# One transformer block pair on one core: the mixer's work put in another order, with the SSD beside the input projections and attention beside memory panels and half of w_out

## The chip, the core and the metric

The kernel runs on one core of a Trainium2 chip. The metric is the device time of one execution in microseconds (us), here the median of three executions. PE is the matrix engine, ACT the scalar engine, DVE the vector engine, POOL the general-purpose engine, SP the queue that issues the loads.

## What is computed

Two blocks on 256 tokens of width 1024, all in fp32. The change lies in the first block's second stage, the hybrid mixer:

```python
proj = u @ w_in
q, k, v, z, xs, bm, cm, dt_raw = jnp.split(proj, np.cumsum(IN_SPLITS)[:-1], axis=-1)
...
o_att = stick_breaking_attention(heads(q), heads(k), heads(v))
o_att = rmsnorm(o_att, attn_norm_g)
...
xbc = lax.conv_general_dilated(
xbc = jax.nn.silu(xbc + conv_b)
dt = jax.nn.softplus(dt_raw.astype(jnp.float32) + dt_bias.astype(jnp.float32))
y = ssd_chunked(xs, dt, a, bmat, cmat)
y = y + d_skip.astype(jnp.float32)[:, None] * xs.astype(jnp.float32)
y = y.reshape(b_, s_, SSD_WIDTH) * jax.nn.silu(z.astype(jnp.float32))
y = rmsnorm(...)
return jnp.concatenate([o_att, o_ssd], axis=-1) @ w_out
```

The SSD (a state-space layer) works on two chunks of 128 tokens; for each it needs a decay matrix for each of 16 heads, a product of it with the scaled inputs, and a state carried from chunk 0 to chunk 1. Attention has 16 heads, taken in 8 pairs. Behind the mixer comes attention to a memory of 256 rows, whose key and value projections (kv0 to kv3) depend on the memory alone.

## The kernel before

All weights come as one stream of blocks of 128x1024 floats, through a ring of four slots, in the order in which PE uses them. Each block is split for precision: ACT rounds it into a high part (L438), DVE subtracts to get the low part (L824), and PE makes three products (L1382, L1383, L1384). ACT may split a block only when PE has used the one four places ahead of it. So each engine carries a list of splits between its other instructions, and each engine works its list in order. Nothing but these hand-written lists and the semaphores sets the order.

A panel is four blocks, 512 output columns. A panel kept by features takes 24 matmuls of 256 columns in a block, one kept by tokens 12 matmuls of 512 columns; a block of w_out also takes 12 of 512 columns. The eleven panels of w_in fill one of two lower PSUM pairs in turn; ACT and DVE copy half of each out. The upper half of PSUM (columns 2048 to 4095) is used by attention, by the SSD's decay rows and by the accumulator of w_out.

The mixer runs so: six panels (q, k, v); then ten turns of a loop over head pairs, in each of which PE does scores, suffix sums and weighted values for three neighbouring pairs and two blocks of the other panels (xs, B, C, z), while ACT and DVE do softplus, the mask and the exponentials and split two blocks; then the dt product (48 matmuls of 16 columns), panels kv1 and kv2 with the convolution on DVE (L1045, L1042); then the SSD: transposes of B and xs, the decay rows (`row_sums`, L1577 and L1580), their exponentials on ACT (L638), the masking on DVE (L1065), the products within a chunk (L1623), the state (L1613, L1628); POOL scales the inputs by heads (L349, L359). Then come the two norms ahead of w_out (`prenorm`: squares, scale, transposes, high and low copies), the 16 blocks of w_out, panel kv3 and the norm behind.

## Time and profile before

| what | value |
|---|---|
| median of 3 executions | 1933.75 us (1932.42 to 1943.19) |
| the profiled execution | 1937.38 us, its span 1935.7 us |
| mean granted clock of PE in it | 0.945 of full speed |
| busy share of the span | PE 91%, DVE 60%, ACT 49%, POOL 6% |
| the mixer in the span | from 241.2 to 593 us |

The profile is of one execution. "PEclk" is the clock that PE was granted, 1.00 being 2.4 GHz and 0.50 being 1.2 GHz. A matmul's printed duration overlaps the next one's; what one costs is the distance between starts. A fp32 product that isn't split shows as two instructions of half the work each.

### The profile page before, as it was taken

Reading aid. Unit: us, or ns where it says so; the run is one execution under the profiler, and the core shown is the slowest. Engines: PE = TensorE matmul, PEld = TensorE weight load, DVE = VectorE, ACT = ScalarE, POOL = GpSimd, SP = SyncE. Lnnn points to the kernel's source line nnn. Section 1 sums busy time; section 2 is a strip of 40 time slices with the busy share of each in tenths; the row PEclk is TensorE's granted clock in tenths of the full one; section 3 lists DMA queues with packets and bytes.
Section 4 is the critical chain, followed back from the end, with each engine's and each line's share of the span. In section 5 each row is a group of like instructions: output and inputs, shape, how many; then the busy total and the mean of one; then the engine's idle time right before and its main releaser. Section 6 shows DMA issues by size and latency. Waiting matters only on the chain.

```text
span 1935.7 us, 30402 instructions
## 1 busy us (share of the span) xinstructions
PE 1758.8 (91%) x10352; PEld 1556.6 (80%) x10352; DVE 1168.2 (60%) x1695; ACT 942.3 (49%) x1470; POOL 125.4 (6%) x108
## 2 busy tenths in 40 slices
PE   5999899997498799997977999897999999999998
PEld 4887798885387578787966999897999988888887
DVE  4554645655344445445674469997888876666664
ACT  5443535543444444435533345454666665544554
POOL 0000000002000000000001001121222210000000
PEclk9999999997598889998977999998999999999999
DMA  5554544222044245553513534544444446565553
GB/s 191 188 186 157 182 166 146 95 87 87 0 163 153 76 145 183 172 185 105 199 56 114 169 122 161 170 149 137 135 137 140 141 141 199 193 194 195 191 191 128
DMA packets 78795, 286.76 MB, mean 148 GB/s; under 512 B 8848, under 2 KB 9104, under 8 KB 78608
## 3 DMA queue, kind: packets, MB, share of 16 engines
q1 hardware_dynamic: 77872, 282.27, 44.0%
q0 software_dynamic: 864, 3.67, 0.6%
q8 instruction: 41, 0.67, 0.1%
q14 instruction: 18, 0.15, 0.0%
HBM read 284.86 MB, written 1.05 MB: 148 GB/s over the span
## 4 chain that ended last, share of the span: by engine, by line
PE 79%; DVE 13%; ACT 5%; issue 2%; DMA 0%; ACTq 0%; DVEq 0%; SPq 0%
PE ps L1382 24%; PE ps L1383 23%; PE ps L1384 23%; DVE w_low L824 3%; PE ps L1795 3%; DVE xT_low L861 1%; ACT w_high L438 1%; DVE digit_hot L1275 1%; PE ps L1623 1%; DVE gate_sum L1280 1%; PE ps L1518 1%; ACT xn L461 1%; PE ps L1446 0%; PE ps L1760 0%; PE ps L1646 0%
## 5 line engine op out<-in xcount | busy, mean ns | idle before, releaser
L824 DVE TENSOR_TENSOR w_low<-ring,w_high 128x1024 fp32r<-128x1024 f32 x532 | 648.7, 1223 | 480.9 <-ACT w_high L438 480.7
L438 ACT ACTIVATE w_high<-ring 128x1024 fp32r<-128x1024 f32 x532 | 558.8, 1054 | 425.4 <-PE ps L1384 425.0
L1382 PE MATMUL ps<-xT_high,w_high 128*128 128x256 f32 x1600 | 468.7, 293 | 35.0 <-DVE w_low L824 18.0
L1383 PE MATMUL ps<-xT_high,w_low 128*128 128x256 f32 x1600 | 461.0, 288 | 0.0
L1384 PE MATMUL ps<-xT_low,w_high 128*128 128x256 f32 x1600 | 461.0, 288 | 0.0
L1382 PEld LDWEIGHTS ps<-xT_high,w_high 128*128 128x128 f32 x1600 | 315.2, 197 | 38.5 <-DVE w_low L824 18.3
L1383 PEld LDWEIGHTS ps<-xT_high,w_low 128*128 128x128 f32 x1600 | 315.3, 197 | 0.0
L1384 PEld LDWEIGHTS ps<-xT_low,w_high 128*128 128x128 f32 x1600 | 314.5, 197 | 0.0
L1382 PE MATMUL ps<-w_high,xT_high 128*128 128x512 f32 x480 | 192.3, 401 | 10.3 <-DVE memT_low L861 4.9
L1382 PE MATMUL ps<-w_high,expert_w_high 128*128 128x512 f32 x512 | 200.1, 391 | 0.0
L1383 PE MATMUL ps<-w_high,expert_w_low 128*128 128x512 f32 x512 | 200.0, 391 | 0.0
L1384 PE MATMUL ps<-w_low,expert_w_high 128*128 128x512 f32 x512 | 200.0, 391 | 0.0
L1383 PE MATMUL ps<-w_high,xT_low 128*128 128x512 f32 x480 | 189.6, 395 | 0.0
L1384 PE MATMUL ps<-w_low,xT_high 128*128 128x512 f32 x480 | 189.2, 394 | 0.0
L801 ACT ACTIVATE expert_w_high<-expert_w 128x256 fp32r x124 | 51.9, 419 | 164.8 <-PE ps L1384 164.8
L1382 PEld LDWEIGHTS ps<-w_high,xT_high 128*128 128x128 f32 x480 | 91.7, 191 | 29.9 <-DVE memT_low L861 5.3
L1382 PE MATMUL ps<-w_high,hT_high 128*128 128x512 f32 x272 | 109.2, 401 | 7.1 <-DVE hT_low L861 2.9
L1384 PEld LDWEIGHTS ps<-w_low,expert_w_high 128*128 128x128 f32 x512 | 96.6, 189 | 20.2
L1382 PEld LDWEIGHTS ps<-w_high,expert_w_high 128*128 128x128 f32 x512 | 96.6, 189 | 20.0 <-issue 0.2
L1383 PEld LDWEIGHTS ps<-w_high,expert_w_low 128*128 128x128 f32 x512 | 96.4, 188 | 20.0
L1384 PE MATMUL ps<-w_low,hT_high 128*128 128x512 f32 x272 | 108.3, 398 | 0.0
L1383 PE MATMUL ps<-w_high,hT_low 128*128 128x512 f32 x272 | 108.3, 398 | 0.0
(330 smaller groups left out, 2056.6 us busy)
## 6 DMA issues: line engine op xcount, KB each, us to landing
ring<-in_stream SPq DMA_DIRECT2D x532, 512.0 KB, 3.3
row_gain<-in_rows POOLq DMA_DIRECT2D x4, 512.0 KB, 4.3
h<-in_x SPq DMA_DIRECT2D x1, 1024.0 KB, 4.9
mem_sb<-in_mem SPq DMA_DIRECT2D x1, 1024.0 KB, 9.8
keys_sb<-in_keys POOLq DMA_DIRECT2D x1, 1024.0 KB, 5.3
out<-result SPq DMA_DIRECT2D x2, 512.0 KB, 2.6
last_gain<-in_rows POOLq DMA_DIRECT2D x1, 512.0 KB, 5.1
cols<-in_cols SPq DMA_DIRECT2D x1, 78.5 KB, 4.6
```

The lines of the kernel that those rows point to most:

```text
L438: act.activation(WH[:, n % SLOTS, :], RING[:, n % SLOTS, :], ACT.Copy).then_inc(w_high, 1)
L461: act.activation(XN[:, tt, g * w:g * w + w], src[:, tt, g * w:g * w + w], ACT.Square, accum_out=STAT[:, n:n + 1]).then_inc(sq_done, 1)
L801: act.activation(WTH[:, v % 4, :], slot, ACT.Copy).then_inc(wt_high, 1)
L824: dve.tensor_tensor(WL[:, n % SLOTS, :], RING[:, n % SLOTS, :], WH[:, n % SLOTS, :].bitcast(F32), ALU.subtract).then_inc(w_split, 1)
L861: dve.scalar_tensor_tensor(low[:, k0 + kt, :], XT_PS[:, kt, :], COLS[:, GAIN_COL[gain] + kt:GAIN_COL[gain] + kt + 1], high[:, k0 + kt, :]. ...
L1275: dve.tensor_tensor(HOT[:, p, :, :], CDIGF[:, tt, p, :].unsqueeze(2).to_broadcast([P, 128, 16]), IOTA[:, 0:16].unsqueeze(1).to_broadcast([ ...
L1280: chain(dve.tensor_copy(GSUM[:, tt, 8:16].unsqueeze(2), CTOP[:, tt, :, 0:1]))
L1382: pe.matmul(out, high, w_hi, start=start, stop=False, skip_group_check=True)
L1383: pe.matmul(out, low, w_hi, start=False, stop=False, skip_group_check=True)
L1384: return pe.matmul(out, high, w_lo, start=False, stop=stop, skip_group_check=True)
L1518: pe.matmul(C_PS[:, h, 0:384], FROM[:], by_head(SPL, k)[:, h, :], start=True, stop=False)
L1795: last = pe.matmul(PS[:, o:o + P], OB[:, g % 2, j, :], OA[:, g % 2, j, :], start=True, stop=True)
```

## The change

The order of w_in's panels becomes xs (2), B and C (1), q, k, z, v (2 each), and w_out's rows for the SSD come before those for attention. The convolution's taps are put between the splits of the second and third panel and of the fourth; the dt product follows the third. The SSD's pieces are put between single blocks of panels 4 to 7, in PSUM's upper half, and the decay rows, exponentials and masks are done in halves of eight heads. The SSD's norm is transposed in the upper half between blocks of panels 9 and 10. The attention loop follows, with the last two blocks of w_in, then kv1 and kv2, then six blocks of w_out beside it; w_out accumulates in the lower half. Attention's norm comes behind the first eight blocks of w_out, the other eight follow. In the diff `step(n, count)` splits blocks n+4 on, `panel(n)` copies panel n out, `mix(n, blocks)` does blocks of panel n on PE. Line numbers in the new file differ.

```diff
+    XT_HI = PS[:, 2048:4096].rearrange("p (k t) -> p k t", k=KT)
+    ACC_LO = PS[:, 0:2048].rearrange("p (t n) -> p t n", t=TT)
...
+    KV_PAIR = [PAIR[0], PAIR[1], PAIR[0], PS[:, 2048:3072]]
...
-    Z = R[:, 9:11, :].rearrange("p a (t n) -> p a t n", t=TT)
+    XBC = R[:, 0:3, :].rearrange("p a (b t) -> p (a b) t", t=SEQ)
+    QT = R[:, 3:5, :].rearrange("p a (b t) -> p (a b) t", t=SEQ)
+    KTT = R[:, 5:7, :].rearrange("p a (b t) -> p (a b) t", t=SEQ)
...
+            pool.wait_ge(conv_done, 12)
+            def adt(tt):
                 pool.tensor_tensor(AU[:], SS[:, 12, tt * 16:tt * 16 + 16].unsqueeze(2).to_broadcast([P, 16, P]),
                                    UPTO[:].unsqueeze(1).to_broadcast([P, 16, P]), ALU.mult).then_inc(au_ok, 1)
-                pool.wait_ge(xs_sb, 2 * (tt + 1))
-                per_head(XD[:, tt, :], XSN[:, tt, :], SS[:, 10, tt * 16:tt * 16 + 16]).then_inc(xd_ok, 1)
-                if tt == 0:
...
+            adt(0)
+            pool.wait_ge(xs_sb, 2)
+            per_head(XD[:, 0, :], XSN[:, 0, :], SS[:, 10, 0:16]).then_inc(xd_ok, 1)
+            pool.wait_ge(dt_a, 4)
+            pool.wait_ge(xd_ok, 1)
+            per_head(XDD[:], XD[:, 0, :], SS[:, 15, 0:16]).then_inc(xd_ok, 1)
+            pool.wait_ge(xs_sb, 4)
+            per_head(YS[:, 0, :], XSN[:, 0, :], SMALL[:, 32:48]).then_inc(yz_ok, 1)
+            pool.wait_ge(row_ps, 2)
+            adt(1)
+            per_head(XD[:, 1, :], XSN[:, 1, :], SS[:, 10, 16:32]).then_inc(xd_ok, 1)
+            per_head(YS[:, 1, :], XSN[:, 1, :], SMALL[:, 32:48]).then_inc(yz_ok, 1)
...
+        step(12)
...
+        step(13, 2)
...
+        conv_silu(0)
+        conv_silu(1)
+        step(15)
+        panel(3)
+        step(16)
+        conv_silu(2)
+        step(17, 2)
+        tokens_out(0)
+        step(19)
+        panel(4)
+        tokens_out(1)
+        step(20, 2)
+        decay(0, 0)
+        step(22)
+        decay(0, 1)
+        step(23)
+        panel(5)
+        step(24, 3)
+        act.wait_ge(st_ps, 1)
+        act.activation(ST[:], PS[:, 3072:4096], ACT.Copy).then_inc(st_ok, 1)
+        step(27)
+        panel(6)
+        decay(1, 0)
+        step(28)
+        decay(1, 1)
+        step(29, 3)
+        panel(7)
+        gate_silu(0)
+        step(32, 3)
+        panel(8)
+        gate_silu(1)
+        step(35)
+        prenorm(3, YS, "ssd", YTH, groups=2, ready=lambda tt: act.wait_ge(y_done, tt + 1),
+                middle=lambda: step(36, 2), between=lambda: step(38, 2), ps=XT_HI)
+        panel(9)
+        act.preload_act_table_set("natural_log_exp_and_others")
...
+        for k in range(10):
+            attention_half(k)
+            if k <= 6:
+                step(42 + 2 * k, 2)
+            elif k <= 8:
+                step(49 + k)
+            if k == 0:
+                panel(10)
+            elif k in (2, 4):
+                kv_evac(k // 2)
+        prenorm(4, AO, "attn", ATH, ready=lambda tt: act.wait_ge(o_done, 8),
+                middle=lambda: step(58), between=lambda: step(59), ps=XT_HI)
...
+        for j in range(4):
+            step(4 + j)
+            conv(0, j)
...
+        for j in range(4):
+            step(8 + j)
+            conv(1, j)
+        panel(2)
+        dve.wait_ge(evac_a, EVAC["w_in"] + 3)
+        dve.wait_ge(evac_d, EVAC["w_in"] + 3)
+        conv(2, 0)
...
+        step(13)
+        conv(2, 2)
...
+        step(14)
+        conv(2, 3)
+        step(15)
+        panel(3)
+        step(16, 2)
...
+        step(18)
+        tokens_out(0)
+        step(19)
+        panel(4)
+        tokens_out(1)
+        step(20, 2)
         dve.wait_ge(cb_ok, 2)
-        for tt in range(TT):
-            dve.wait_ge(xs_ps, tt + 1)
-            dve.tensor_copy(XSN[:, tt, 512:1024], PS[:, 512:1024]).then_inc(xs_sb, 1)
-        for tt in range(TT):
-            dve.wait_ge(lm_ok, tt + 1)
-            for g in range(2):
-                m = LM[:, 8 * g:8 * g + 8, :]
-                last = dve.tensor_tensor(m, m, CBM[:, tt, g, :].unsqueeze(1).to_broadcast([P, 8, P]), ALU.mult)
-            last.then_inc(m_ok, 1)
-            dve.wait_ge(y_ps, tt + 1)
-            dve.wait_ge(yz_ok, tt + 1)
+        masked(0, 0)
+        step(22)
+        masked(0, 1)
+        step(23)
+        panel(5)
+        step(24, 2)
+        dve.wait_ge(y_ps, 1)
+        dve.wait_ge(yz_ok, 1)
+        dve.tensor_tensor(YS[:, 0, :], YS[:, 0, :], PS[:, 2048:3072], ALU.add).then_inc(y_used, 1)
+        step(26, 2)
+        panel(6)
+        masked(1, 0)
+        step(28)
+        masked(1, 1)
+        step(29, 2)
+        dve.wait_ge(y_ps, 2)
+        dve.wait_ge(yz_ok, 2)
+        chain(dve.tensor_tensor(YS[:, 1, :], YS[:, 1, :], PS[:, 2048:3072], ALU.add))
+        step(31)
+        panel(7)
+        dve.wait_ge(y_ps, 3)
+        chain(dve.tensor_tensor(XDD[:].rearrange("p (h d) -> p h d", d=64),
+                                PS[:, 3072:4096].rearrange("p (h d) -> p h d", d=64),
+                                SS[:, 15, 16:32].unsqueeze(2).to_broadcast([P, 16, 64]), ALU.mult))
+        dve.tensor_tensor(YS[:, 1, :], YS[:, 1, :], XDD[:], ALU.add).then_inc(y_used, 1)
+        step(32, 3)
+        panel(8)
...
+        for n in range(3):
+            mix(n)
...
+        mix(3, range(0, 2))
+        pe.wait_ge(masks_ok, 5)
+        pe.wait_ge(dt_d, 3)
+        pe.matmul(PS[:, 3136:3168], UPTO[:], SS[:, 12, :], start=True, stop=True)
...
+        mix(3, range(2, 4))
+        mix(4, range(0, 2))
+        pe.wait_ge(cv_done, 3)
+        pe.wait_ge(acs_ok, 1)
...
+        mix(4, range(2, 3))
+        xs_tokens(0)
+        mix(4, range(3, 4))
+        pe.wait_ge(xs_sb, 2)
+        xs_tokens(1)
+        mix(5, range(0, 1))
+        pe.wait_ge(xs_sb, 4)
+        row_sums(0, 0)
+        mix(5, range(1, 2))
+        pe.wait_ge(cb_ok, 2)
+        row_sums(0, 1)
+        mix(5, range(2, 4))
+        mix(6, range(0, 1))
+        within(0)
+        mix(6, range(1, 2))
+        pe.wait_ge(lm_ok, 2)
+        pe.wait_ge(xd_ok, 2)
+        state_product(lambda g: BN[:, g, :], XDD).then_inc(st_ps, 1)
+        mix(6, range(2, 3))
+        pe.wait_ge(y_used, 1)
+        row_sums(1, 0)
+        mix(6, range(3, 4))
+        pe.wait_ge(st_ok, 1)
+        row_sums(1, 1)
+        mix(7, range(0, 3))
+        within(1)
+        mix(7, range(3, 4))
+        state_product(lambda g: CV[:, 10 + g, P:SEQ], ST).then_inc(y_ps, 1)
+        mix(8)
+        mix(9)
+        turn_tile(3, 0, XT_HI)
+        mix(10, range(0, 1))
+        turn_tile(3, 1, XT_HI)
+        mix(10, range(1, 2))
+        pe.wait_ge(xt_low, 4 * KT)
...
             if k < 8:
                 scores(k)
             if 1 <= k <= 8:
                 suffix_sums(k - 1)
+            if k == 2:
+                pe.wait_ge(evac_a, EVAC["w_in"] + 11)
+                pe.wait_ge(evac_d, EVAC["w_in"] + 11)
             if k >= 2:
                 weighted_values(k - 2)
...
+            if k == 0:
+                mix(10, range(2, 4))
+            elif k <= 4:
+                if k == 1:
+                    pe.wait_ge(evac_a, EVAC["w_in"] + 10)
+                    pe.wait_ge(evac_d, EVAC["w_in"] + 10)
+                kv_panel((k + 1) // 2, range((k + 1) % 2 * 2, (k + 1) % 2 * 2 + 2))
+            elif k <= 6:
+                if k == 5:
+                    kv_out(1)
+                    kv_out(2)
+                rows_product("w_out", 16, YTH, YTL, ACC_LO, range(2 * k - 10, 2 * k - 8))
+            elif k <= 8:
+                rows_product("w_out", 16, YTH, YTL, ACC_LO, range(k - 3, k - 2))
+        rows_product("w_out", 16, YTH, YTL, ACC_LO, range(6, 8))
+        transpose_norm(4, XT_HI)
+        rows_product("w_out", 16, ATH, ATL, ACC_LO, range(8, 16))
```

On PE, behind the decay product of chunk 0, there stood before (`xs_dt,decay` is the product within a chunk, `adt_upto` and `future` are the decay rows):

```order
L1613 MATMUL ps<-xs_dt_decay,b_tokens 128x512 [waits cb_masked_done,xs_dt_ok]
L1613 MATMUL ps<-xs_dt_decay,b_tokens 128x512
L1623 MATMUL ps<-xs_dt,decay 128x64 [waits xs_copied,xs_dt_ok,m_ok]
L1623 MATMUL ps<-xs_dt,decay 128x64 x15
L1577 MATMUL ps<-adt_upto,ones 128x512 [waits decay_exp,adt_upto_ok]
```

And now the same product stands between two blocks of panel 6:

```order
L1512 MATMUL ps<-xT_high,w_high 128x256
L1513 MATMUL ps<-xT_high,w_low 128x256
L1514 MATMUL ps<-xT_low,w_high 128x256
L1694 MATMUL ps<-xs_dt,decay 128x64 [waits xs_dt_ok,m_ok]
L1694 MATMUL ps<-xs_dt,decay 128x64 x15
L1512 MATMUL ps<-xT_high,w_high 128x256 [waits w_split_done]
L1513 MATMUL ps<-xT_high,w_low 128x256
```

A block of 24 matmuls (rows cut here to three) is now queued on either side of it. On DVE the masks of chunk 0 and the sum behind them stood together before:

```order
L1065 TENSOR_TENSOR decay<-decay,cb_masked 128x1024 [waits decay_exp]
L1065 TENSOR_TENSOR decay<-decay,cb_masked 128x1024
L1070 TENSOR_TENSOR ssd_out<-ssd_out,ps 128x1024 [waits yz_ok,y_psum]
L1078 TENSOR_TENSOR ssd_out<-ssd_out,projections 128x1024 [waits z_silu,dve_chain]
L1065 TENSOR_TENSOR decay<-decay,cb_masked 128x1024 [waits decay_exp]
```

and now they stand so, from the first mask on:

```order
L1103 TENSOR_TENSOR decay<-decay,cb_masked 128x1024 [waits decay_exp,cb_masked_done]
L889 TENSOR_TENSOR w_low<-ring,w_high 128x1024 [waits w_high_done]
L1103 TENSOR_TENSOR decay<-decay,cb_masked 128x1024 [waits decay_exp]
L889 TENSOR_TENSOR w_low<-ring,w_high 128x1024 [waits w_high_done]
L934 COPY projections<-ps 128x512 [waits w_used]
L889 TENSOR_TENSOR w_low<-ring,w_high 128x1024 [waits w_high_done] x2
L1171 TENSOR_TENSOR ssd_out<-ssd_out,ps 128x1024 [waits yz_ok,y_psum]
```

Four splits and a panel's copy moved in between, so that a mask that waits holds splits behind it.

## Rows read from the trace of the kernel before

**Rows 1.** Page, chain that ended last: share of the span by engine.

```profile
PE 79%; DVE 13%; ACT 5%; issue 2%; DMA 0%; ACTq 0%; DVEq 0%; SPq 0%
```

**Rows 2.** Windows over the stretch: us, busy (x instructions) by engine, PEclk, DMA share, GB/s.

```profile
241.20:312.00 70.80, 70.69 (x480) 66.60 (x480) 32.26 (x29) 26.85 (x29) 0.00 (x0) 0.96 0.53 177
315.00:408.00 93.00, 86.79 (x589) 76.59 (x590) 56.22 (x62) 47.56 (x62) 0.00 (x0) 0.98 0.30 101
453.50:528.40 74.90, 40.90 (x147) 28.56 (x146) 27.84 (x43) 32.50 (x77) 13.16 (x6) 0.63 0.07 23
528.40:585.60 57.20, 57.19 (x240) 46.81 (x240) 26.37 (x29) 24.16 (x31) 0.59 (x1) 0.95 0.45 153
```

**Rows 3.** Timeline of PE: start us, us, what; weight-block matmuls, features then tokens.

```profile
309.69 0.39 PE L1382 MATMUL ps<-w_high,xT_high 128*128 128x512 f32 x1
311.50 0.39 PE L1384 MATMUL ps<-w_low,xT_high 128*128 128x512 f32 x1
...
326.13 0.28 PE L1383 MATMUL ps<-xT_high,w_low 128*128 128x256 f32 x1
331.64 0.28 PE L1384 MATMUL ps<-xT_low,w_high 128*128 128x256 f32 x1
```

**Rows 4.** Timeline of PE: the dt product and the SSD's own matmuls.

```profile
412.53 0.17 PE L1382 MATMUL ps<-w_dt_high,xT_high 128*128 128x16 f32 x1
417.86 0.56 PE L1382 MATMUL ps<-memT_high,w_high 128*128 128x256 f32 x1
...
457.91 1.04 PE L1595 MATMUL ps<-ident,conv_out 128*128 128x128 f32 x8
...
469.71 7.09 PE L1623 MATMUL ps<-xs_dt,decay 128*128 128x64 f32 x32 [2.00 <-DVE decay L1065]
479.67 1.02 PE L1577 MATMUL ps<-adt_upto,ones 128*128 128x512 f32 x2
480.52 1.02 PE L1580 MATMUL ps<-future,ident 128*128 128x512 f32 x2
...
498.58 3.73 PE L1628 MATMUL ps<-state,conv_out 128*128 128x512 f32 x4
```

**Rows 5.** Windows behind the dt product and in the decay product, columns as rows 2.

```profile
417.80:421.10 3.30, 3.30 (x17) 3.30 (x17) 1.87 (x9) 0.46 (x2) 0.56 (x1) 0.50 0.06 22
469.00:477.00 8.00, 7.29 (x33) 7.29 (x34) 0.82 (x2) 0.27 (x1) 5.79 (x3) 0.50 0.00 0
```

**Rows 6.** Timeline: attention's first score product, its last copy.

```profile
314.99 0.92 PE L1506 MATMUL ps<-projections 64*128 64x256 f32 x4 [3.10 <-DVE projections L867]
...
407.19 0.38 ACT L596 ACTIVATE attention_out<-ps 128x256 f32<-128x256 f32 x1 [0.17 <-PE ps L1533]
```

**Rows 7.** Groups by line, 241 to 600 us: busy, mean ns | idle before, releaser.

```profile
L824 DVE TENSOR_TENSOR w_low<-ring,w_high 128x1024 fp32r<-128x1024 f32 x74 | 89.5, 1223 | 98.4 <-ACT w_high L438 98.3
L438 ACT ACTIVATE w_high<-ring 128x1024 fp32r<-128x1024 f32 x73 | 76.1, 1056 | 95.0 <-PE ps L1384 95.0
```

**Rows 8.** Timeline: POOL's products, and DVE's masking beside and without them.

```profile
461.98 1.90 POOL L349 TENSOR_TENSOR xs_dt_decay<-xs_dt,ssd_small 128x1024 f32<-128x1024 f32 x1
463.84 3.61 POOL L359 TENSOR_TENSOR adt_upto<-ssd_small,upto 128x2048 f32<-128x2048 f32 x1
...
465.16 4.50 DVE L1065 TENSOR_TENSOR decay<-decay,cb_masked 128x1024 f32<-128x1024 f32 x2 [3.42 <-ACT decay L638]
489.28 2.36 DVE L1065 TENSOR_TENSOR decay<-decay,cb_masked 128x1024 f32<-128x1024 f32 x2 [9.96 <-ACT decay L638]
```

**Rows 9.** Timeline: the norm ahead of w_out, ACT and DVE.

```profile
507.38 1.06 ACT L461 ACTIVATE xn<-attention_out 128x1024 f32<-128x1024 f32 x1 [18.13 <-DVE ssd_out L1078]
508.54 1.28 ACT L467 ACT_TABLE_LOAD   x1
514.45 3.02 ACT L481 ACTIVATE hT_high<-ps,cols 128x256 fp32r<-128x256 f32 x8 [1.57 <-PE ps L1390]
...
512.91 0.75 DVE L854 TENSOR_SCALAR xn<-attention_out,stat 128x1024 f32<-128x1024 f32 x1 [0.27 <-ACT stat L474]
```

More of the change, by code:

```diff
@@ L940, in between @@
                 split(b, 3)
[L942 removed]
+            prenorm(k, H, gain, between=between, begun=True, ps=ps)
             split(b + 3, 1)
@@ L992, in _, with step, panel @@
         b = BASE["w_in"]
[L993 to L1002 removed]
+        def step(n, count=1):
+            split(b + PB + n, count)
+        def panel(n):
+            evac("w_in", mixer_dst, n, PAIR[n % 2])
         def both(heads):
@@ L1460, in ffn_up, with rows_product @@
             pe.wait_ge(ht_low, e + FFN_PANELS)
-        def rows_product(stage, kts, high=HTH, low=HTL):
-            for kt in range(kts):
+        def rows_product(stage, kts, high=HTH, low=HTL, acc=ACC, part=None):
+            for kt in part or range(kts):
                 n = BASE[stage] + kt
```

407 lines of the change are left out of this document (189 added, 218 removed).

## The prediction

> **What bounds the kernel now.** I read the page's chain first: 79% of what ended last is PE [rows 1]. Then I cut the stretch that the change touches into windows. Up to 312 us PE is busy without a break. The attention loop, 315 to 408 us, keeps it busy for 86.8 of 93 us. From 453.5 to 528.4 us it is busy for 40.9 of 74.9 us, at a mean clock of 0.63, while no weights are loaded [rows 2]: there the SSD and the norms hand one thing on from engine to engine, and nothing else is queued. That is what the new order can fill. The projections themselves are bound by PE: DVE's split of a block takes 1.22 us and ACT's 1.06 us [rows 7], PE's three products 2.7 to 2.9 us.
>
> **PE's own prices.** Between the starts at 326.13 and 331.64 us lie 46 matmuls of a features panel, 0.12 us each, so 24 make a block of 2.87 us. From 309.69 to 311.50 us lie 8 of a tokens panel, 0.226 us each, so 12 make 2.72 us [rows 3]. The dt product lasts from 412.53 to 417.86 us, 5.3 us. Two decay-row instructions start 0.85 us after the two before them, so the 32 (16 such pairs) cost 13.8 us at full clock. The product within a chunk took 7.1 us, but at a clock of 0.50 [rows 4, 5], so about 3.55 us at full clock, 7.1 us for two chunks. The state's product took 3.73 us in the stretch whose mean clock was 0.63; I take it as at half clock too, so both (state out and in) cost 3.6 us (7.3 if not). Sixteen transposes of 128 columns cost about 1.8 us (eight last 1.04 us with the overlap [rows 4]), once for xs and once for a norm; B, C and the small sums together I take at 1.7 us.
>
> **The change, summed.** The stretch compared goes from the first block of w_in at 241.2 us to the last block of kv3 at 585.6 us: 344.4 us [rows 2].
>
> (1) Up to attention's first score product, PE has 28 features blocks (80.4), 14 tokens blocks (38.1), dt (5.3), B, C and sums (1.7), xs (1.8), decay rows (13.8), within (7.1), states (3.6) and the SSD norm's transposes (1.8). The slow start stays as it is: 16 features and 8 tokens blocks should take 67.7 us and the window has 70.8, so 3.1 us. Together 156.7 us.
>
> (2) Waits of PE there, found by walking the lists of the engines with those durations. Behind dt, PE has two blocks (5.7 us) while DVE goes through about ten small operations, a split (1.2) and four taps, some 8 us: 2.6 us. Before B and C are transposed, ACT's last silu stands behind two splits and a table load of 1.28 us [rows 9]: 0.4 us. At the end the SSD norm's low copies come 1.7 us after the second block of panel 10. Everywhere else the pieces of work ahead cover the chain: for instance the decay rows of half a chunk are followed by a block or two (2.9 to 5.7 us), and ACT needs 2.1 us for eight exponentials plus a split. Sum 4.7 us. The convolution is hidden: four taps and a split last as long as a block, and the ring lets DVE fall several microseconds behind.
>
> (3) The clock. Behind the dt product's 16-column matmuls it was 0.50 for 3.3 us though PE was busy throughout [rows 5], a loss of 1.65 us. I take three such falls that nothing absorbs (behind each product within a chunk, whose matmuls have 64 columns, and at the norm); the one behind dt falls into the wait of (2). 5.0 us.
>
> (4) POOL. Its decay input took 3.61 us from 463.84; DVE's two masks, begun at 465.16, lasted 4.50 us, and 2.36 us when POOL was idle [rows 8]: DVE stood for as long as POOL was still at work. In the new order POOL's seven products (two of 3.6, five of about 1.9 us, 16.7 us in all) run beside DVE's splits and masks. Most splits have slack of several microseconds by the four slots of the ring. The critical ones are the copy of xs for the second chunk (about 1.8 us late) and the first masks (2.4 us late). 4.2 us. The bounds are 0 and 16.7.
> The Trainium skill (GPSIMD Engine Reference, Specifications) says why: POOL's SBUF interfaces are shared with VectorE, and it names contention with DVE instructions that have two SBUF inputs. Every split is one. The trace agrees for the masks; by the rule taken to its end all 16.7 us would land on PE, which is in the third rival.
>
> So attention's first score product comes 156.7 + 4.7 + 5.0 + 4.2 = 170.6 us after the start.
>
> (5) The attention loop had 92.6 us, from 314.99 to the end of its last copy at 407.57 [rows 6]. It is a cycle of latencies, not of PE work: two ACT splits, a DVE split, softplus back and forth, the mask, an exponential, the copy. That cycle stays in seven turns, whatever PE's two blocks belong to. In turn 7 one split less (1.06 + 1.22, of which about 1.4 matters) and in turn 8 one block less before the last weighted values: I take 2.9 us off. 89.7 us.
>
> (6) Attention's norm. Before, the first square started at 507.38 and the eight high copies ended at 517.47 (514.45 + 3.02); the low copies end just over 1 us later, 11.2 us in all [rows 9]. Two splits now stand in it, 1.06 us each, one hidden by DVE's scale of 0.75 us and the transposes. 12.3 us. PE has only two blocks of w_out and its transposes to put against it, so PE idles about 5.5 us in it.
>
> (7) Eight blocks of w_out and four of kv3, 32.6 us, plus a cold start of 2.8 us (20 blocks took 57.2 us where 54.4 were due [rows 2]). 35.4 us.
>
> Sum 170.6 + 89.7 + 12.3 + 35.4 = 308.0 us against 344.4: 36.4 us less. The junction behind it (to 593 us) and all later stages are the same instructions. The profiled execution took 1937.4 us, 3.6 over the median, so 1901.0 in a like execution and **1897 us** as a median. Nothing is added but three more table loads on ACT (eight for five) of 1.28 us [rows 9], which lie in ACT's slack while PE has a block or more in hand; uncovered they would cost 3.8 us. No DMA is added, and the loads move from bursts to a steady pace: the w_in stage ran at 177 GB/s [rows 2] and needs no more now.
>
> **The rivals.**
> (a) The forecast, 1881 to 1912 us: chance 0.55.
> (b) The hand-overs hide better: POOL holds nothing (4.2), no fall of the clock is paid (5.0 and 2.8 at w_out), half of (2) goes. 14 us more, about 1883 us or lower. For it: DVE is busy in less than two thirds of the time even with its new work. Against it: the fall behind dt was real. 0.2.
> (c) The lists are too tight. A mask or sum that waits holds the splits behind it, and the ring is four blocks deep. If all of POOL's work holds DVE (12.5 us more) and ten hand-overs come 0.8 us later than I walked them, 20 us are lost: 1917 us. For it: every split in that stretch has two SBUF inputs, and there are thirteen places where PE waits for another engine between blocks. Against it: before a wait PE has 2.9 us or more of other work. 0.2.
> (d) Slower, by the clock alone: if the many short products hold PE at 0.50 instead of letting it recover in 3.3 us, each 2 us so spent cost one. It takes 36.4 us of loss, that is 73 us more at half clock out of the 170 up to attention, to reach the time before, and 100 us at half clock would give 1897 + 50 = 1947 us. Against it: rows 5 show the recovery during plain blocks, and plain blocks stand between all pieces. 0.03.
> (e) The stall only moves: the loop of attention turns takes as much longer as the SSD is shorter, since its w_out blocks and norms depend on each other. That is some 35 us in ten turns, for which I see no wait; 1930 us or so. 0.02.
>
> **Numbers.** The likeliest is 1897 us. Leaving out (d), (e) and the outer parts of (b) and (c) gives 1879 to 1918 for 8 in 10; own range of (a) as above. A difference under 0.5% (9.7 us) can't be told from none. Faster by more than that: (a), (b), (c), 0.95; same 0.02; slower 0.03.
>
> **What would show it.** After: the window of w_in and SSD, 241.2 us to the first score product, should last 165 to 177 us with PE idle under 15 us; the masks should last over 2 us each where POOL's products lie beside them; 0.50 should appear behind dt and both products within a chunk for about 3 us; the loop from there to the last attention copy about 90 us; a gap of 5 to 6 us in PE in attention's norm; kv3 ends near 549 us. I am wrong if PE waits for `w_low` inside panels 4 to 8 for more than 10 us in sum, or if the turns of attention last more than 11 us.

## The result and the profile after

The changed kernel takes **1903.69 us** (median of 4 runs, 1899.2 to 1904.5) against 1933.93 us for the kernel before in the same session: ratio **0.9827**, 95% interval 0.9805 to 0.9849. Two more sessions gave 0.9797 (0.9752 to 0.9842) and 0.9831 (0.9812 to 0.9851). The prediction was 1897 us, 1879 to 1918. The profiled execution's span is 1902.3 us, 33.4 less than before.

Windows of the profile after, with the columns of [rows 2]: from the first block of w_in to attention's first score product, attention's loop, its norm, w_out's second half with kv3, and the rest.

```profile
241.79:415.09 173.30, 168.08 (x1038) 150.78 (x1038) 102.00 (x138) 76.69 (x121) 19.44 (x7) 0.91 0.37 127
415.09:507.07 91.98, 80.59 (x467) 65.77 (x468) 56.07 (x62) 47.52 (x62) 0.00 (x0) 0.98 0.29 98
507.07:519.12 12.05, 7.09 (x39) 5.66 (x37) 7.18 (x16) 11.05 (x19) 0.00 (x0) 0.94 0.37 131
519.12:554.56 35.44, 35.44 (x144) 28.74 (x144) 16.57 (x21) 15.66 (x23) 0.59 (x1) 0.92 0.38 130
554.56:1902.30 1347.74, 1246.60 (x7686) 1124.62 (x7686) 869.02 (x1316) 679.11 (x1099) 104.76 (x81) 0.96 0.44 153
```

The first four lines sum to 312.8 us where the prediction had 308.0 and the kernel before 344.4: 31.6 us less. The last line is code that the change leaves as it was; 1.8 us of the 33.4 are there or ahead of the stretch.

Every number below comes from one account. I cut a stretch into windows of 1 us and multiply PE's busy time in each by one minus its granted clock; the sum is the **loss** to the clock. The stretch's length less PE's busy time is **idle**, and what is left is **work** at full clock. Over the whole stretch:

| | length | idle | loss | work |
|---|---|---|---|---|
| before, 241.2 to 585.6 | 344.4 | 45.8 | 26.6 | 271.9 |
| after, 241.8 to 554.6 | 312.8 | 21.6 | 19.2 | 271.9 |

The work is the same to a tenth of a microsecond. The chain that ended last is PE for 78% of the span, DVE for 14% and ACT for 5% ([rows 1]: 79, 13, 5), so what binds has not changed. The change took 24.2 us of idle PE and 7.4 us of slow clock out, and nothing else. Idle time of PE in the profile after, 241 to 555 us, by what ended it (us, times, longest):

```profile
PE ps L1646 <- ACT attention_out L613: 9.0, 6, 4.3
PE ps L1512 <- DVE xT_low L928: 4.6, 1, 4.6
PE ps L1512 <- DVE attention_outT_low L928: 3.5, 1, 3.5
PE ps L1717 <- DVE ssd_small L1139: 2.6, 1, 2.6
PE ps L1694 <- DVE decay L1103: 1.9, 1, 1.9
```

The second line lies ahead of w_in's first block and is not in the account. The wait for `ssd_small` is the sums of the log decays behind dt; the wait for `decay` is the first product within a chunk. What led to the first of the two stands in ACT's and DVE's timelines (the dt product ends at 286.71 us, the wait lasts from 295.08 to 297.63):

```profile
292.13 1.06 ACT L450 ACTIVATE w_high<-ring 128x1024 fp32r<-128x1024 f32 x1 [9.64 <-PE ps L1514]
293.09 0.21 ACT L656 ACTIVATE ssd_small<-ssd_small 128x32 f32<-128x32 f32 x1
```

ACT idles for 9.64 us, since in its list the exponential of the dt chain stands behind the split of a block whose ring slot PE frees only with its first block behind dt. So the chain starts when PE has used that block, and lasts 5.5 us from there (292.13 to 297.63); PE has one block (2.95 us) to put against it, and 2.6 us are left. In a2, a later profile of the same kernel, it is 287.64 to 293.15 us and 2.7 us.

Then the slow clock, in four windows of the same profile (the second of them is the part of the fall that lies within the dt product) and in the one behind turn 8 of attention:

```profile
282.80:292.30 9.50, 9.50 (x46) 9.50 (x46) 2.87 (x9) 0.17 (x1) 0.00 (x0) 0.50 0.15 56
282.11:286.71 4.60, 4.60 (x24) 4.60 (x24) 3.17 (x9) 0.36 (x2) 0.00 (x0) 0.50 0.33 119
300.00:302.50 2.50, 2.50 (x14) 2.50 (x14) 0.48 (x3) 0.00 (x0) 0.00 (x0) 0.50 0.47 184
345.00:353.20 8.20, 8.20 (x40) 8.20 (x40) 1.03 (x1) 0.00 (x0) 0.00 (x0) 0.50 0.40 128
496.00:502.00 6.00, 4.88 (x21) 3.70 (x22) 1.23 (x1) 1.92 (x3) 0.00 (x0) 0.72 0.23 87
```

In the first of them PE has no gap at all and still runs at 0.50 (1.2 of 2.4 GHz) for 9.5 us. The fall begins within the dt product, whose 16-column matmuls last from 279.15 to 286.71 us: the granted clock is 1.00 up to 282.11 us and 0.50 from there to 292.35, 10.2 us in all. [Rows 5] had 3.3 us, from the end of the same product on. The timeline shows POOL beside DVE, as [rows 8] did before, and PE behind them; the mask at 369.29 us has no POOL beside it:

```profile
332.77 3.61 POOL L366 TENSOR_TENSOR adt_upto<-ssd_small,upto 128x2048 f32<-128x2048 f32 x1 [7.72 <-PE ps L1679]
336.34 2.89 POOL L358 TENSOR_TENSOR xs_dt<-xs_tokens,ssd_small 128x1024 f32<-128x1024 f32 x1
...
333.99 3.47 DVE L1103 TENSOR_TENSOR decay<-decay,cb_masked 128x1024 f32<-128x1024 f32 x1 [2.33 <-ACT decay L632]
337.39 2.92 DVE L889 TENSOR_TENSOR w_low<-ring,w_high 128x1024 fp32r<-128x1024 f32 x1
340.24 2.92 DVE L1103 TENSOR_TENSOR decay<-decay,cb_masked 128x1024 f32<-128x1024 f32 x1
369.29 1.23 DVE L1103 TENSOR_TENSOR decay<-decay,cb_masked 128x1024 f32<-128x1024 f32 x1 [0.72 <-ACT decay L632]
...
343.21 2.12 PE L1694 MATMUL ps<-xs_dt,decay 128*128 128x64 f32 x10 [1.90 <-DVE decay L1103]
```

And the places of [rows 6, 9] now: first score product, the wait of turn 9, the last copy, attention's norm with two splits in it.

```profile
415.09 0.71 PE L1634 MATMUL ps<-projections 64*128 64x256 f32 x4 [0.77 <-DVE ssd_outT_low L928]
497.12 1.60 PE L1646 MATMUL ps<-softplus,from 128*128 128x384 f32 x2 [4.34 <-ACT attention_out L613]
...
506.69 0.38 ACT L613 ACTIVATE attention_out<-ps 128x256 f32<-128x256 f32 x1 [0.66 <-PE ps L1661]
508.27 1.28 ACT L479 ACT_TABLE_LOAD   x1
510.86 1.04 ACT L450 ACTIVATE w_high<-ring 128x1024 fp32r<-128x1024 f32 x1
513.56 1.04 ACT L450 ACTIVATE w_high<-ring 128x1024 fp32r<-128x1024 f32 x1
514.97 3.02 ACT L495 ACTIVATE attention_outT_high<-ps,cols 128x256 fp32r<-128x256 f32 x8 [0.37 <-PE ps L1519]
```

### The profile page after: what moved, and what is told of

It reads as the page before. It is cut to its first block, busy times and chain, and to the rows that moved or that the text cites. A ratio compares the mean times of both kernels' runs of the same rounds, so it can differ in the third digit from the quotient of the medians.

```text
span 1902.3 us, 30191 instructions
## 1 busy us (share of the span) xinstructions
PE 1749.4 (92%) x10352; PEld 1551.8 (82%) x10352; DVE 1173.0 (62%) x1695; ACT 945.3 (50%) x1474; POOL 128.9 (7%) x108
## 4 chain that ended last, share of the span: by engine, by line
PE 78%; DVE 14%; ACT 5%; issue 2%; DMA 0%; ACTq 0%; SPq 0%; DVEq 0%
PE ps L1512 24%; PE ps L1514 23%; PE ps L1513 23%; DVE w_low L889 4%; PE ps L1954 3%; ACT w_high L450 1%; DVE xT_low L928 1%; DVE digit_hot L1405 1%; DVE gate_sum L1410 1%; PE ps L1646 1%; PE ps L1694 1%; PE ps L1579 0%; PE ps L1919 0%; PE ps L1805 0%; DVE softplus L1041 0%
## 5 line engine op out<-in xcount | busy, mean ns | idle before, releaser
L1512 PE MATMUL ps<-xT_high,w_high 128*128 128x256 f32 x1600 | 471.2, 295 | 33.9 <-DVE w_low L889 16.7
L1512 PEld LDWEIGHTS ps<-w_high,xT_high 128*128 128x128 f32 x480 | 91.7, 191 | 30.4 <-DVE memT_low L928 5.3
L1514 PEld LDWEIGHTS ps<-w_low,xT_high 128*128 128x128 f32 x480 | 91.4, 190 | 19.6
L1513 PEld LDWEIGHTS ps<-w_high,xT_low 128*128 128x128 f32 x480 | 91.7, 191 | 18.9 <-issue 0.5
L1491 DVE TENSOR_TENSOR expert_w_low<-expert_w,expert_w_high 128x256 fp32r<-128x256 f32 x124 | 52.7, 425 | 82.2 <-ACT expert_w_high L866 82.2
```

The costliest lines, as they stand in the source:

```text
L1491: dve.tensor_tensor(WTL[:, v % 4, :], slot, WTH[:, v % 4, :].bitcast(F32), ALU.subtract).then_inc(wt_low, 1)
L1512: pe.matmul(out, high, w_hi, start=start, stop=False, skip_group_check=True)
L1513: pe.matmul(out, low, w_hi, start=False, stop=False, skip_group_check=True)
L1514: return pe.matmul(out, high, w_lo, start=False, stop=stop, skip_group_check=True)
```

## The experiments

All edits are to the changed kernel. The columns of the account are for the stretch from w_in's first block to attention's first score product, in each kernel's own profile; "loop" goes from there to attention's last copy. Times are medians, ratios against the kernel before in the same session.

| run | median | ratio (95%) | length | idle | loss | work | loop |
|---|---|---|---|---|---|---|---|
| changed | 1903.7 | 0.9827 (0.9805–0.9849) | 173.3 | 5.2 | 15.0 | 153.1 | 92.0 |
| a1, again | 1897.0 | 0.9797 (0.9752–0.9842) | 168.6 | 5.3 | 9.7 | 153.5 | 92.0 |
| a2, a third time | 1902.5 | 0.9831 (0.9812–0.9851) | 168.0 | 5.4 | 9.1 | 153.6 | 92.0 |
| e7 SSD in one piece | 1917.9 | 0.9901 (0.9879–0.9922) | 189.5 | 14.6 | 21.3 | 153.5 | 92.0 |
| e1 w_out behind | 1918.4 | 0.9916 (0.9894–0.9938) | 168.0 | 5.4 | 9.0 | 153.6 | 90.0 |
| e2 dt spread | 1900.2 | 0.9814 (0.9797–0.9831) | 169.4 | 7.7 | 8.2 | 153.5 | 92.0 |
| e8 dt early | 1896.2 | 0.9786 (0.9752–0.9820) | 163.5 | 3.2 | 6.4 | 153.8 | 94.4 |
| e6 within spread | 1899.1 | 0.9802 (0.9768–0.9836) | 164.9 | 5.4 | 5.6 | 153.8 | 92.0 |
| e3 POOL late | 1895.2 | 0.9777 (0.9736–0.9819) | 162.8 | 3.5 | 5.7 | 153.6 | 94.1 |
| e10 POOL twice | 1903.9 | 0.9839 (0.9817–0.9861) | 173.5 | 7.1 | 13.1 | 153.2 | 91.7 |
| e4 turn 7 | 1901.5 | 0.9820 (0.9796–0.9843) | 168.6 | 5.4 | 9.8 | 153.5 | 90.3 |
| e9 three edits | 1888.3 | 0.9763 (0.9749–0.9778) | 157.6 | 1.4 | 2.3 | 153.9 | 90.6 |

**e7: the new order of panels, but the SSD in one piece.** In all three engines' lists the splits and blocks between the SSD's pieces move behind it:

```diff
-        mix(5, range(0, 1))
...
         row_sums(0, 0)
-        mix(5, range(1, 2))
...
         row_sums(0, 1)
-        mix(5, range(2, 4))
-        mix(6, range(0, 1))
         within(0)
...
         state_product(lambda g: CV[:, 10 + g, P:SEQ], ST).then_inc(y_ps, 1)
-        mix(8)
+        for n in range(5, 9):
+            mix(n)
```

> The new order of panels stays (convolution panels and dt first, q, k, z, v behind), but the SSD from its decay rows to the state's product runs in one serial piece between panel 4 and panel 5, with no block of a panel inside it. My theory: the time comes from the blocks that stand between the SSD's pieces. In the kernel before, the same pieces stood alone from about 453.5 to 500 us; so the stretch to attention's first score product grows from 173.3 us by 30 to 45 us, PE idles there 25 to 35 us instead of 5.2, the clock is 0.50 in most of it, and the kernel takes 1930 to 1945 us: no faster than before. Rival: the order of panels alone (conv first, so that the convolution hides) is worth most of it; then the kernel stays under 1915 us.

1917.9 us: between the two theories, on neither side. The stretch grew by 16.2 us where 30 to 45 were expected, and PE idles 14.6 us in it instead of 25 to 35. The SSD's piece has these waits in e7:

```profile
PE ps L1682 <- DVE decay L1099: 8.3, 2, 4.8
PE ps L1664 <- DVE xs_tokens L1093: 2.8, 1, 2.8
```

and these are those of the kernel before from 453 to 529 us:

```profile
PE ps L1390 <- ACT xn L469: 14.2, 2, 9.1
PE ps L1623 <- DVE decay L1065: 8.7, 2, 6.7
PE ps L1601 <- DVE xa_v L867: 3.1, 1, 3.1
PE ps L1613 <- POOL xs_dt_decay L349: 2.9, 1, 2.9
```

The waits for `decay` (8.7 and 8.3 us) and for an input of the SSD (`xs_dt_decay` 2.9, `xs_tokens` 2.8 us) are the SSD's own and are still there in e7; the norms (14.2 us) and the copy of `xa_v` (3.1 us) were no matter of its pieces. So the gain has two halves: 1934.9 to 1917.9, 17.0 us, is the rest of the change, that is the new order of panels together with w_out's blocks beside attention; and 14 to 21 us, by the three sessions of the changed kernel, is the blocks between the pieces. e7 doesn't part the two things in the first half; e1 below takes the second of them away and loses as much again. No run has the order of the panels alone. By the account those blocks are worth 9.2 us of idle time (14.6 to 5.4) and 6 to 12 us of loss.

**e1: w_out's first eight blocks behind attention's norm.**

```diff
-            if k <= 6:
+            if k <= 4:
                 step(42 + 2 * k, 2)
-            elif k <= 8:
-                step(49 + k)
...
         transpose_norm(4, XT_HI)
+        rows_product("w_out", 16, YTH, YTL, ACC_LO, range(0, 8))
         rows_product("w_out", 16, ATH, ATL, ACC_LO, range(8, 16))
```

> The first eight blocks of w_out leave attention's turns 5 to 8 and stand behind attention's norm, ahead of the other eight; all else is the changed kernel. My theory: the turns are a cycle of latencies, so turns 5 to 8 get shorter only by the splits that leave them (1 to 2.3 us a turn, 4 to 9 us), while the 21.8 us of PE work is no longer hidden: attention's loop 84 to 88 us instead of 91.8, the last kv3 block 12 to 18 us later than in the changed kernel, 1915 to 1922 us. Rival: the turns are bound by PE with its blocks; then each turn without blocks gets shorter by their 5.4 us, the loop lasts 70 to 75 us, and the time stays within 4 us of 1903.

1918.4 us, as the theory had it, 15 to 21 us over the changed kernel's three sessions. But the loop became only 2.0 us shorter (92.0 to 90.0, where 84 to 88 was expected):

```profile
408.63:498.61 89.98, 69.49 (x392) 57.07 (x392) 49.46 (x56) 41.73 (x56) 0.00 (x0) 0.86 0.22 71
```

PE is busy for 69.5 us of 90, at 0.86: with the blocks gone 20.5 us are idle (11.4 before the edit), and the turns' own matmuls lose 8.2 us to the clock (1.7 before). A turn is a cycle of latencies, and the w_out blocks in it are almost free, since they also keep PE's clock up.

**a1 and a2: the changed kernel again.**

> The changed kernel as it is, once more. From its first block of w_in to attention's first score product its first profile had 173.3 us, of which 5.2 us PE idle and 15.0 us lost to the clock; two kernels whose instructions are the same up to there (one w_out block moved in turn 7, w_out behind the norm) had 168.6 and 168.0 us, with the same idle time but 9.8 and 9.0 us lost. Theory: how long the clock stays at half after the dt product (3 or 9 us) and behind the wait for the masks (0, 6 or 8 us) is not set by the program; then this profile has idle 5.2 to 5.4 us, full-clock work 153 to 154 us, and any loss from 9 to 15 us. Rival: the loss belongs to this program, since its instructions lie elsewhere in memory than those of the two others; then it is 15 us again, at the same places.

> The changed kernel a third time, beside the next two. By the account so far the stretch to attention's first score product is 153.5 us of work at full clock, 5.3 us of idle PE and a loss to the clock that came out as 15.0 and 9.7 us: 168 to 174 us again, and 164 to 165 if both optional falls stay short; median 1896 to 1904 us.

Idle time and work came out as in the first profile, and the loss did not: 15.0, 9.7, 9.1 us. These windows of a1 lie over the same instructions as the 282.80 and 345.00 rows above:

```profile
282.00:292.00 10.00, 10.00 (x50) 10.00 (x51) 2.97 (x9) 0.39 (x1) 0.00 (x0) 0.53 0.16 53
336.00:356.00 20.00, 18.10 (x130) 15.77 (x129) 12.68 (x9) 7.71 (x15) 5.59 (x2) 1.00 0.33 106
```

The fall behind the masks is not there at all (1.00). Summed over windows of 2 us, as the time at half clock that gives each window's mean, the fall behind dt lasted 3.4 us (a2, e1, e3, e6) or 10.2 us (the first profile, a1, e4, e7, e10), and nothing between; the one at the wait for the masks was absent (a1, e4, e6), 6.8 us long (a2, e1, e2, e8, e10) or 10.2 (the first). The rival, that the loss belongs to this program's place in memory, falls with a1 and a2, whose program is the first one's. The Trainium skill (TensorE: Matmul & The Clock Gate, Part 1) says that the hardware watches PE's activity in windows that run on whatever the kernel does, so that the moment at which the clock changes varies from run to run. The page gives half a microsecond for it, at a kernel's start. The three profiles of one program agree that it varies, but not in size: one fall lasted 3.4 or 10.2 us.

What goes with the length can be read from the traces, by the moment at which the clock first rose to 1.00 in the stretch. In the five profiles with the long fall that was 5.8 to 6.2 us after w_in's first block had begun, and the fall began within the dt product; in the four with the short one it was 4.5 to 4.6 us after it, and the fall began with the product's end. The first profile, a1, a2, e1 and e4 have the same instructions up to there. Among them a1 (5.8 us) and e4 (5.9) agree in every fall, and so do a2 (4.6) and e1 (4.5); the first (6.2) stands apart. So where the clock's changes fell against the program's work at the start goes with all that came later. No run moved it on purpose, so this is a match in nine profiles and not a shown cause.

**e2: the dt product spread over panel 2's blocks.**

```diff
-        for tt in range(TT):
-            for kt in range(KT):
...
+            for kt in (2 * blk, 2 * blk + 1):
+                for ft in range(4):
+                    if ft % 2:
...
                         last = product(PS[:, 3072 + tt * 16:3088 + tt * 16], ...)
+                    used = product(PAIR[0][:, ft * SEQ:(ft + 1) * SEQ], WH[:, s, w], WL[:, s, w],
```

> The 16 triples of the dt product, with 16 columns each, stand singly between the matmuls of the four blocks of panel 2 instead of in one run behind them. Theory of the clock: it fell because PE did nothing but 16-column matmuls for 5.3 us; spread, no stretch is without wide matmuls, so 0.50 from 282.8 to 292.3 us goes and the first score product comes 4 to 5 us earlier (168 to 169 us after the start). Rival one: the fall has nothing to do with the form of the work; it stays, and the stretch stays 172 to 175 us. Rival two: the clock recovers, but DVE, which now takes panel 2's taps and the dt chain at once, keeps PE waiting at the row sums up to 4 us longer than the 2.55 us now, and nothing is won.

Windows of e2 where the fall behind dt had been, and behind it:

```profile
280.00:292.00 12.00, 9.97 (x85) 9.77 (x83) 9.21 (x21) 5.28 (x7) 0.00 (x0) 0.99 0.35 125
290.00:300.00 10.00, 5.04 (x28) 5.07 (x29) 7.60 (x22) 1.40 (x3) 0.00 (x0) 0.66 0.32 106
```

The fall is gone: 0.99, where each of the nine profiles with dt in one run has a fall. And rival two came about: the wait for the chain is 5.0 us instead of 2.6, since panel 2 and dt now end together, and the clock falls behind that wait. 169.4 us against 168.0 to 173.3: nothing won.

**e8: the same, one panel earlier.** Panel 1 takes the dt product, and the chain's operations go among the taps and splits of panel 1:

```diff
-        for n in range(3):
+        for n in range(1):
             mix(n)
...
-        mix(3, range(0, 2))
+        mix(2)
...
         pe.wait_ge(dt_d, 3)
         pe.matmul(PS[:, 3136:3168], UPTO[:], SS[:, 12, :], start=True, stop=True)
```

> The dt product spread as in e2, but one panel earlier (in panel 1), with its chain on ACT and DVE among the taps and splits of panels 1 and 2, and the sums of the log decays behind panel 2. Theory: in e2 the clock stayed up where dt had been, but the wait for its chain was 5.0 us instead of 2.6, and a fall came behind that wait. With a whole panel to hide the chain, wait and both falls go: PE idles 2.7 us up to the first score product, the loss is 2.6 (cold start) to 8 us, and the stretch lasts 159 to 164 us (173.3, 168.6 and 168.0 so far); kernel 1892 to 1898 us. Rival: DVE's taps and the chain now stand in the way of the splits of panel 3, and PE waits for weights instead (2 to 6 us more idle): 168 us or more.

The window over both falls and the wait of the changed kernel, in e8:

```profile
282.00:302.00 20.00, 19.93 (x167) 19.73 (x165) 19.72 (x41) 11.87 (x15) 1.44 (x1) 1.00 0.53 179
```

PE is busy for 19.93 of 20 us at full clock. The cold start ended 5.9 us after the first block, as in the profiles with the long fall. The stretch takes 163.5 us; what is left of the loss is the cold start and one fall of 6.8 us at the wait for the masks. The rival's wait for weights didn't come.

**e6: the narrow matmuls of the first chunk spread over a block.**

```diff
-        within(0)
-        mix(6, range(1, 2))
...
+        for i in range(8):
...
+            for h in (2 * i, 2 * i + 1):
+                last = pe.matmul(PS[:, 2048 + h * 64:2048 + (h + 1) * 64], LM[:, h, :], ...)
...
+            used = product(PAIR[0][:, ft * SEQ:(ft + 1) * SEQ], WH[:, s, w], WL[:, s, w],
```

> The 16 products with 64 columns of the first chunk stand two by two between the matmuls of the block behind them, instead of in one run. Both the wait of 1.9 us for the masks ahead of them and all the rest stay. Theory: the fall of the clock there follows the wait, not the narrow products; it comes or not as in the four profiles so far (0 to 8 us lost half), at the same place. Rival: it comes from the narrow products, and never with them spread: loss 0 between 340 and 360 us.

No loss between 340 and 360 us. By itself that settles nothing: a1 and e4, with the products in one run, had none there either. But a2 and e1 ran as e6 did up to this wait: the cold start ended 4.5 to 4.6 us after the first block, the fall behind dt was the short one, and the wait began 95.9 us after the first block in all three. Here is a2 with its fall, which began 2.4 us into the products, and e6 from the end of the wait on:

```profile
341.18:348.01 6.83, 6.83 (x34) 6.83 (x34) 0.43 (x1) 0.00 (x0) 0.00 (x0) 0.50 0.43 148
...
338.50:360.00 21.50, 21.50 (x127) 16.60 (x128) 8.42 (x9) 6.64 (x13) 0.00 (x0) 1.00 0.31 102
```

a2 and e1, with the products in one run, had 6.8 us of it each, and e6 none. That speaks for the rival. In e3 and e9 the products stand in one run without a wait ahead of them, and there is no fall either. So no profile has a fall here without both, the wait and the narrow products in one run behind it, though a1 and e4 had both and no fall; e6 is one profile, and this is a hint, not a proof. In time there is nothing: 1899.1 us lies amid the changed kernel's sessions.

**e3: POOL's second chunk behind the first masks.**

```diff
             pool.wait_ge(row_ps, 2)
+            pool.wait_ge(m_ok, 2)
             adt(1)
```

> POOL's decay input and its two products for the second chunk wait until DVE has made both masks of the first chunk. Theory of the shared hold: the split begun at 323.9 us (2.2 us) and the two masks (3.5 and 2.9 us) that lay beside POOL's products take 1.2 us each; the wait of 1.9 us for the masks ahead of the product within a chunk goes, and with it the fall of the clock that followed it in three of four profiles; first score product after 161 to 167 us. Rival: the decay input for the second chunk now comes too late, and the wait moves to the row sums of the second chunk (2 to 5 us). Second rival: DVE was not held by POOL but by its own operands; masks and splits stay as long as they were.

The timeline of e3:

```profile
336.03 4.46 POOL L366 TENSOR_TENSOR adt_upto<-ssd_small,upto 128x2048 f32<-128x2048 f32 x1 [15.13 <-DVE decay L1104]
...
329.85 1.23 DVE L1104 TENSOR_TENSOR decay<-decay,cb_masked 128x1024 f32<-128x1024 f32 x1 [2.33 <-ACT decay L633]
334.66 1.23 DVE L1104 TENSOR_TENSOR decay<-decay,cb_masked 128x1024 f32<-128x1024 f32 x1 [0.83 <-ACT decay L633]
335.80 1.22 DVE L890 TENSOR_TENSOR w_low<-ring,w_high 128x1024 fp32r<-128x1024 f32 x1
336.94 0.69 DVE L935 COPY projections<-ps 128x512 f32<-128x512 f32 x1
338.36 3.21 DVE L890 TENSOR_TENSOR w_low<-ring,w_high 128x1024 fp32r<-128x1024 f32 x1 [0.73 <-ACT w_high L451]
```

Both masks take 1.23 us (3.47 and 2.92 before the edit), PE's 1.9 us wait is gone, and no fall comes between 336 and 360 us: 162.8 us, and nothing waits later for POOL. The split at 323.9 us, which lies beside the first chunk's products, stayed at 2.2 us; there my expectation was careless, since the edit holds back only the second chunk's products. The copy at 336.94 has its input in PSUM and takes 0.69 us with POOL in the middle of a product; the split at 338.36 has both inputs in SBUF and takes 3.21.

**e10: POOL makes the second chunk's decay input twice.**

```diff
+            pool.tensor_tensor(AU[:], SS[:, 12, 16:32]..., UPTO[:]..., ALU.mult).then_inc(masks_one, 1)
+            pool.wait_ge(masks_one, 7)
             adt(1)
```

> POOL makes the decay input of the second chunk twice, one behind the other (3.6 us more POOL work beside DVE's first masks and split; the result is the same). If DVE with two SBUF inputs stands whenever POOL is in a product, and POOL when DVE is: the first mask lasts 3.5 us as before, the split and the second mask end 1.7 us later (one product of 3.6 us in the place of one of 1.9), PE's wait for the masks grows from 1.9 to 3.6 us, and the stretch by 2 us beside what the clock does. Rival: only the time of POOL's products counts, not their place: all 3.6 us come on top, wait 5.5 us. Second rival: DVE is slowed by a share and not stopped; the split lasts 2.4 us and the wait stays near 2 us.

```profile
331.85 3.61 POOL L378 TENSOR_TENSOR adt_upto<-ssd_small,upto 128x2048 f32<-128x2048 f32 x1 [7.72 <-PE ps L1682]
335.54 4.48 POOL L366 TENSOR_TENSOR adt_upto<-ssd_small,upto 128x2048 f32<-128x2048 f32 x1
...
333.07 3.47 DVE L1106 TENSOR_TENSOR decay<-decay,cb_masked 128x1024 f32<-128x1024 f32 x1 [2.33 <-ACT decay L635]
336.47 4.63 DVE L892 TENSOR_TENSOR w_low<-ring,w_high 128x1024 fp32r<-128x1024 f32 x1
341.02 2.92 DVE L1106 TENSOR_TENSOR decay<-decay,cb_masked 128x1024 f32<-128x1024 f32 x1
...
343.99 5.68 PE L1697 MATMUL ps<-xs_dt,decay 128*128 128x64 f32 x32 [3.60 <-DVE decay L1106]
```

The wait is 3.60 us, as expected to the tenth: 3.61 in the place of a product of 1.90 us. The two engines alternate. POOL's product ends at 335.46; the mask begun at 333.07 ends at 336.54, 1.08 us later; POOL's next one, begun at 335.54, ends at 340.02, 3.5 us after the mask; the split begun at 336.47 ends at 341.10, 1.08 us after that. Each stops the other whole, and neither is slowed by a share. The Trainium skill (SBUF — State Buffer, SBUF: two separate sides) calls the ports that the two engines share an exclusive lock, and the trace agrees, with 3.47, 4.63 and 4.48 us for operations of 1.23, 1.22 and 3.61.

**e4: both w_out blocks in turn 7, none in turn 8.**

```diff
-            if k <= 6:
+            if k <= 7:
                 step(42 + 2 * k, 2)
-            elif k <= 8:
-                step(49 + k)
```

> Two blocks of w_out in attention's turn 7 and none in turn 8, instead of one in each. Theory: PE idles 4.3 us at the start of turn 9 for the copy of turn 8, because turn 8 had only one block against the same chain, and the clock then falls to 0.7; turn 7 has a chain that lasts as long whatever PE does. With both in turn 7, that turn takes 2 us longer at most, turn 8 2 to 3 us less, and the last copy comes 0 to 2 us earlier. Rival: the blocks do not matter at all where they lie, since the chain through ACT and DVE sets each turn: last copy within 0.5 us of the changed kernel's, the wait for the copy grows by 2.7 us to 7 us. Both are too small to be seen in the time; they are read from the profile.

The loop took 90.3 us, 1.7 less. Idle time did not change (11.5 us against 11.4), so my reason was wrong: the wait only moved (4.3 us at turn 9 became 1.6 us there and 3.1 us later). What went is the fall of the clock behind it within the loop (1.7 us to 0.2), and it went no further than past the last copy: it came at 499.6 us, where the loop ends at 500.1. So from the loop's end to kv3's end 46.9 us stand against 46.3 to 47.6 in the changed kernel.

**e9: e8, e3 and e4 together.**

> dt spread in panel 1 with its chain a panel earlier, POOL's second chunk behind the first masks, and both w_out blocks in attention's turn 7. If the three work side by side: PE idles 1.3 us up to the first score product, the only loss is the cold start's 2.6 us, the stretch lasts 153.6 + 1.3 + 2.6 = 157.5 us; attention's loop 90 to 92 us; median 1886 to 1891 us, 8 to 12 us under the changed kernel in the same call. Rival: with the falls taken away at these places they come at another (the score of idle and loss is kept elsewhere), the sum of loop and norms grows by what was won, and the median stays within 4 us of the changed kernel's.

**1888.34 us** (1888.11 to 1890.13) beside 1902.49 for the changed kernel in the same session: 14.2 us less, with intervals of the ratio that don't touch. Its stretch up to the first score product:

```profile
240.94:398.55 157.61, 156.25 (x1038) 139.06 (x1038) 99.63 (x138) 76.25 (x121) 20.05 (x7) 0.99 0.43 140
```

157.6 us where 157.5 were expected; the largest wait left in it is 0.8 us. The rival, that the falls turn up elsewhere, is refuted: 294.8 us to the end of kv3 against 307.6 in a2. It is the best version found. That the three edits together gave 14.2 us and not the 8 to 12 expected is within what the changed kernel's own medians differ by (1897.0 to 1903.7).

## Why the prediction was right, and where it wasn't

The direction, the size and case (a) of the prediction were right: 307.6 and 306.9 us of stretch in two profiles and 312.8 in the first, 308.0 predicted. By its steps:

- **(1) PE's own work** was 156.7 us, 3.1 of it the cold start, so 153.6 of work. The twelve profiles have 153.1 to 153.9, and the cold start cost 3.1, 2.9 and 2.3 us in the three of the changed kernel. Priced from rows 3 and 4, the sum came out to 0.5 us.
- **(2) Waits, 4.7.** The one behind dt is 2.6 as forecast, but that is luck. I had DVE busy for some 8 us behind dt against 5.7 us of PE's blocks (which leaves 2.3, not 2.6). In fact the chain ended 10.9 us behind dt (10.1 in a2) and PE's blocks took 8.4 us (7.3), because ACT's exponential was held until PE had used its first block. The last silu costs nothing (0.4 predicted), the norm's low copies 0.8 (1.7). So 3.4.
- **(3) The clock, 5.0: this term was mis-sized, by its sizes and its places.** Beyond the cold start the loss was 11.9, 6.8 and 6.8 us in the three profiles. None came behind the second product within a chunk nor at the norm. The fall at dt, which I took to vanish in the wait of (2), didn't: it slowed the block that the chain itself waited for, so the chain ended later by as much and the wait stayed whole (2.6 us beside 10.2 us at 0.50, 2.7 us beside 3.4 us). It lasted up to 10.2 us where rows 5 had 3.3, nearly half of it within the dt product, and a second fall stood behind the wait.
- **(4) POOL, 4.2.** 1.9 us reached PE, shown by e3 (gone) and e10 (3.6). I had charged 1.8 us to the copies of xs, but their input is in PSUM, and such copies aren't stopped by POOL.
- (2) and (4) were 3.6 us too high, (3) 1.8 to 6.9 too low: the sum, 170.6, lies amid 173.3, 168.6 and 168.0. The middle is in part luck.
- **(5) The loop, 89.7: the 2.9 us taken off for fewer blocks in turns 7 and 8 were not there.** 92.0 in all three profiles (92.6 before). I had myself written that the cycle sets the turn, and e1 bears it out: with no block at all in four turns it is 90.0, though 8.2 us of PE's work in it were then lost to the clock. PE idles 4.34 us for the copy of turn 8 instead.
- **(6) and (7)** were 12.3 and 35.4, measured 12.1 and 35.4.
- **Rivals.** (c), that all of POOL's work lands on PE, fell: 1.9 of 16.7 us. (b)'s time was not reached by this kernel, but e9, which takes its costs away, comes to 1888. (d), the clock alone, had the right worry: it is the largest term above the work, 9 to 15 us, but far from the 36 needed. (e) fell, idle time is 24.2 us less.

Of the signs named, the first window (173.3 us, 5.2 idle) and the masks of over 2 us came as said; 0.50 came once behind a product within a chunk and not twice; the gap in attention's norm (5.0 us of idle PE) and the loop (92.0) were near; kv3 ended at 554.6 us instead of 549, and in the two later profiles at 548.2 and 548.6.

The gain's source is shown by the account, e7 and e1: about half from the blocks between the SSD's pieces, and about half from the rest of the new order, in which w_out's blocks beside attention have a large part (e1). How that second half divides is not shown.

What stays open: whether the clock's position at the start of the stretch decides between the short and the long fall or only goes with it; whether a wait and narrow matmuls behind it are both needed for the fall at the masks (e6 and e3 are one profile each); and why the fall behind the wait of turn 9 lasted 10.2 us in e3 and e8, and 3.4 us in the changed kernel, which makes their loops 2 us longer (the same 11.2 us idle, but 4.5 and 4.8 us of loss). Whether the wait behind dt goes when ACT's exponential stands ahead of the split was not tried; e8 moved the whole chain a panel earlier.

## What to carry to other kernels

Split the time of a stretch into work at full clock, idle time and loss to the clock: the work can be summed to 0.5 us from a few matmul prices, and what a reordering can win is only the other two. In this kernel a block of independent matmuls in a latency-bound cycle was worth twice, since it also kept the clock up. Walk a chain through every engine's list: one small operation behind a split that waits for a ring slot ties the chain to PE's own progress, and then PE's work can't hide it. A narrow product is better spread between wide ones, but early enough that the chain behind it has a panel to hide in. Where POOL and DVE both work from SBUF, place POOL's products where DVE copies from PSUM or has nothing due, and count a DVE operation of two SBUF inputs beside them as POOL's remainder plus its own time.

## What the runs showed of the hardware that I had not expected

One program at the same instructions lost 15.0, 9.7 and 9.1 us to the clock in three profiles. From within the dt product on the clock stayed at 0.50 for 10.2 us with PE busy throughout, or from its end on for 3.4 us; behind a wait of 1.9 us it stayed there for 10.2 or 6.8 us, or did not fall at all. Part of a kernel's run-to-run spread may be this: the changed kernel's runs lie up to 12.7 us apart in a session (1891.7 to 1904.5). Over all sessions, the three versions with the dt product spread (e2, e8, e9) have runs 1.7 to 2.0 us apart, and the nine sessions with it in one piece 4.9 to 12.7 us. The falls can be seen only in the one profiled run of each, so the link is strongly suggested and not shown. DVE and POOL stop each other whole in both directions: DVE's mask of 1.23 us took 3.47, and POOL's product of 3.61 us took 4.46 and 4.48.
